# Twelve of the 36 modulation chunks of part one move into the third feed-forward of part two

## The reference, cut to what matters

```python
cond_x = silu(c); cond_c = silu(c_ctx)
mx = split((cond_x @ mod_w[layer] + mod_b[layer])[:, None, :], 9, axis=-1)
mc = split(cond_c @ mod_w[layer] + mod_b[layer], 9, axis=-1)
x  = x  + 0.5 * mx[2] * swiglu(modulate(rms_norm(x),  mx[0], mx[1]), ffn_w_in[layer, 0], ffn_w_out[layer, 0])
xc = xc + 0.5 * mc[2] * swiglu(modulate(rms_norm(xc), mc[0], mc[1]), ffn_w_in[layer, 0], ffn_w_out[layer, 0])
# then the mixer with mx[3..5], then the second feed-forward with mx[6..8]
```

## Time and profile before

| | |
|---|---|
| median of 3 executions | 2864.19 us (2854.37 to 2866.15) |
| the profiled execution: its time, its span | 2856.93 us, 2855.1 us |
| PE busy | 2663.7 us (93%) |
| DVE busy | 1565.7 us (55%) |
| ACT busy | 1078.3 us (38%) |
| HBM read | 390.54 MB, 137 GB/s over the span |
| mean granted TensorE clock | 0.974 |
| part one | about 0 to 1020 us |
| unit (1, 0) | about 2080 to 2460 us |

### The profile page before, as it was taken

One profiled execution on the slowest core, in us unless ns is written; L12 is line 12 of the kernel. 1 busy time (PEld: TensorE's weight loads), 2 busy tenths in 40 slices (PEclk: granted clock), 3 DMA queues, 4 the chain that ended last, 5 costly groups with the idle time before them and its releaser, 6 DMA issues.

```text
span 2855.1 us, 44372 instructions
## 1 busy us (share of the span) xinstructions
PE 2663.7 (93%) x17820; PEld 2325.0 (81%) x17820; DVE 1565.7 (55%) x2307; ACT 1078.3 (38%) x1427; POOL 0.2 (0%) x4
## 2 busy tenths in 40 slices
PE   7999999999999969999998999999999999887997
PEld 6887899888789968877786688787888778876997
DVE  7676665677666564333366553333353423676665
ACT  3354553335455443222241433222232222345443
POOL 0000000000000000000000000000000000000000
PEclk9999999999999989999999999999999999999998
DMA  7655567564557734344432024354534444531563
GB/s 212 198 165 192 177 210 215 154 193 156 188 167 222 213 105 122 106 132 128 133 96 74 1 60 126 106 144 114 145 98 125 139 116 112 114 80 53 144 188 103
DMA packets 591271, 394.54 MB, mean 138 GB/s; under 512 B 52278, under 2 KB 584660, under 8 KB 590932
## 3 DMA queue, kind: packets, MB, share of 16 engines
q1 hardware_dynamic: 591060, 391.63, 47.9%
HBM read 390.54 MB, written 1.05 MB: 137 GB/s over the span
## 4 chain that ended last, share of the span: by engine, by line
PE 76%; DVE 13%; ACT 5%; issue 3%; DMA 2%; DVEq 0%; SPq 0%; ACTq 0%
PE bank L2044 76%; DVE w_lo L1205 4%; ACT w_hi L853 3%; DMA raw<-in_ffn_w_out 2%; DVE xs L1220 1%; DVE t L1220 1%; DVE t L1217 1%; DVE small L1839 1%; DVE h_lo L1220 1%; DVE gates L1213 0%; ACT xs L857 0%; ACT t L857 0%; DVE acc L1213 0%; ACT x_hi L857 0%; DMA raw<-in_w_in 0%
## 5 line engine op out<-in xcount | busy, mean ns | idle before, releaser
L1205 DVE TENSOR_TENSOR w_lo<-raw,w_hi 128x2048 fp32r<-128x2048 f32 (+3 forms) x337 | 687.3, 2040 | 575.8 <-ACT w_hi L853 573.8
L853 ACT CAST w_hi<-raw 128x2048 fp32r<-128x2048 f32 (+3 forms) x337 | 572.9, 1701 | 771.0 <-PE bank L2044 386.7
L2044 PE MATMUL bank<-h_hi,w_hi 128*128 128x512 f32 (+1 forms) x1688 | 590.5, 350 | 25.9 <-DVE h_lo L1220 14.2
L2044 PE MATMUL bank<-h_lo,w_hi 128*128 128x512 f32 (+1 forms) x1688 | 583.1, 345 | 0.0
L2044 PE MATMUL bank<-h_hi,w_lo 128*128 128x512 f32 (+1 forms) x1688 | 582.2, 345 | 0.0
L2044 PE MATMUL bank<-x_hi,w_hi 128*128 128x256 f32 x1344 | 387.8, 289 | 35.8 <-DVE x_lo L1220 13.1
L2044 PEld LDWEIGHTS bank<-h_hi,w_hi 128*128 128x128 f32 x1688 | 321.1, 190 | 79.5 <-issue 23.3
L2044 PE MATMUL bank<-x_lo,w_hi 128*128 128x256 f32 x1344 | 378.8, 282 | 0.0
L2044 PE MATMUL bank<-x_hi,w_lo 128*128 128x256 f32 x1344 | 378.3, 281 | 0.0
L2044 PEld LDWEIGHTS bank<-h_hi,w_lo 128*128 128x128 f32 x1688 | 321.1, 190 | 39.0
L2044 PEld LDWEIGHTS bank<-h_lo,w_hi 128*128 128x128 f32 x1688 | 321.4, 190 | 37.6
(11 more groups left out here) (282 smaller groups left out, 3622.8 us busy)
## 6 DMA issues: line engine op xcount, KB each, us to landing
raw<-in_ffn_w_in SPq DMA_DIRECT2D x176, 512.0 KB
raw<-in_ffn_w_out SPq DMA_DIRECT2D x64, 704.0 KB
raw<-in_w_in SPq DMA_DIRECT2D x40, 1024.0 KB
xs<-in_mod_w SPq DMA_DIRECT2D x36, 1024.0 KB, 7.3
raw<-in_mod_w SPq DMA_DIRECT2D x36, 1024.0 KB
raw<-in_w_ff_in SPq DMA_DIRECT2D x32, 1024.0 KB
raw<-in_w_ff_out SPq DMA_DIRECT2D x32, 1024.0 KB
raw<-in_w_out SPq DMA_DIRECT2D x8, 1024.0 KB
```

Of the source, the lines that this page charges most:

```text
L853: act.copy(w_hi[s][:, w], raw[at % SLOTS][:, w]).then_inc(hi_made, c.did(hi_made))
L1205: dve.tensor_tensor(w_lo[s][:, w], raw[r][:, w], w_hi[s][:, w].bitcast(F32), ALU.subtract).then_inc(lo_made, c.did(lo_made))
L2044: ins = pe.transpose(o, l, r) if transpose else pe.matmul(o, l, r, start=start, stop=stop)
```

## The change

Unit (1, 0) makes twelve modulation chunks in each of its two passes, where it made six, and part one makes twelve in each of its two passes, where it made eighteen. The twelve that move are columns 24 to 35 of layer 1's modulation (in chunks of 256), which the last feed-forward uses. In part one the rest follow each other by three weight chunks (later nine and eight) and the turns come after chunks 23 and 53. In unit (1, 0) a pass now has modulation chunks after k = 1, 2, 3, 4, 5, 6, 8, 10, 12, 14, 15 and 16, and turns after 7 and 18. It had them after 1, 3, 5, 7, 13 and 15 and a turn after 17. Two semaphore counts per pass of part one follow.

```diff
-MOD_AFTER = [6, 8, 10, 13, 16, 18, 20, 22, 24, 26, 28, 30, 32, 34, 40, 42, 44, 47]
+MOD_AFTER = [6, 9, 12, 15, 18, 21, 24, 27, 30, 33, 42, 50]
 MODS1 = len(MOD_AFTER)
-MOD_TURN = (20, 32, 50)
-MOD_GROUPS1 = [(0, 12, 0), (0, 12, 6), (1, 6, 24)]
+MOD_TURN = (23, 53)
+MOD_GROUPS1 = [(0, 12, 0), (0, 12, 6)]
...
-FFN_MOD_AFTER = [1, 3, 5, 7, 13, 15]
-FFN_MOD_TURN = (17,)
-FFN_MODS = {(0, 0): (6, 0, 24), (0, 1): (6, 1, 0), (1, 0): (6, 1, 12), (1, 1): (0, 0, 0)}
+FFN_MOD_AFTER = {0: [], 6: [1, 3, 5, 7, 13, 15], 12: [1, 2, 3, 4, 5, 6, 8, 10, 12, 14, 15, 16]}
+FFN_MOD_TURN = {0: (), 6: (17,), 12: (7, 18)}
+FFN_MODS = {(0, 0): (6, 0, 24), (0, 1): (6, 1, 0), (1, 0): (12, 1, 12), (1, 1): (0, 0, 0)}
...
-        if k in FFN_MOD_AFTER[:FFN_MODS[unit][0]]:
-            out.append(("mod", FFN_MOD_AFTER.index(k)))
+        if k in FFN_MOD_AFTER[FFN_MODS[unit][0]]:
+            out.append(("mod", FFN_MOD_AFTER[FFN_MODS[unit][0]].index(k)))
...
-                        if k in FFN_MOD_TURN[:count // MOD_GROUP]:
+                        if k in FFN_MOD_TURN[count]:
                             mod_turn()
-                        if k in FFN_MOD_AFTER[:count]:
-                            q = FFN_MOD_AFTER.index(k)
+                        if k in FFN_MOD_AFTER[count]:
+                            q = FFN_MOD_AFTER[count].index(k)
```

More of the change, by code:

```diff
@@ L416 @@
             'chunk_used': 72,
-            'd_free': 70,
-            'd_full': 52,
+            'd_free': 63,
+            'd_full': 51,
             'exp_made': 22,
@@ L435 @@
             'm_lo_made': 4,
-            'mod_full': 18,
-            'mod_in': 288,
+            'mod_full': 12,
+            'mod_in': 192,
             'o_hi_made': 9,
@@ L1775, in mod @@
                     for g in range(count // MOD_GROUP):
-                        if k == FFN_MOD_TURN[g]:
+                        if k == FFN_MOD_TURN[count][g]:
                             mod_columns(layer, j, count, first + MOD_GROUP * g)
-                    if k in FFN_MOD_AFTER[:count]:
-                        mod_row(FFN_MOD_AFTER.index(k))
+                    if k in FFN_MOD_AFTER[count]:
+                        mod_row(FFN_MOD_AFTER[count].index(k))
                 def unit_lo(t):
```

## The result

The changed kernel takes 2995.16 us in the median (2994.89 to 3001.81) where the kernel before takes 2862.15: the ratio is 1.0461, with a 95% interval of 1.0441 to 1.0482. The profiled execution took 3001.81 us, with a span of 3000.0, 144.9 us more than the 2855.1 before.

The account below looks back on a forecast made before the run. It took PE as the bound, with loads waiting for slots freed by modulation products. Stalls, clock and moved work, less 2.0 us of old stalls and 12 us in part one, gave +139.3 us: 3003.5 us, range 2950 to 3040.

Parts of the forecast that it names:

- gate/up stalls: Unit (1, 0), mid-chunk: PE waits for an up tile's bank, 5.25 us, five times in each of two passes, 52.5 us.
- chunk 13's: Unit (1, 0), chunk 13: PE waits for a bank evicted behind M14's `w_lo`, 3.4 us, twice, 6.8 us.
- output stalls: Output part of unit (1, 0): PE waits for the residual, 9.4 us, twice in each pass, 37.6 us.
- Clock: PE slower after gaps in unit (1, 0): fourteen stalls by 2.8 us, 39.2 us, plus 1.6 us for two short stalls.
- The check value: Sign that the prediction is right: granted clock of the changed unit (1, 0) near 0.85 in place of 1.00.
- The moved work: Unit (1, 0): twelve more products, 13.2 us of PE, and two more turns, 2.4 us.
- Part one: Twelve products and two turns leave part one: 12 us saved, with bounds of 6 and 34.
- lower of the prediction's own bounds: Whole kernel: 2964 us if the low bounds of clock, loads and part one all fall together.
- the clock stays: Rival, 12%: the stalls in unit (1, 0) come but cost no clock; 2963 us.
- only output steps stall: Rival, 5%: in unit (1, 0) the up tiles' banks come free in time; 2923 us.
- nothing stalls: Rival, 6%: the load is issued before the modulation product ends in unit (1, 0), not slower; 2868 us.
- faster: Rival, 5%: no stall, and part one's waits vanish with their clock; 2846 us, from a saving of 30 us there.

Follow-up runs that it names:

- the run with filler work: Changed kernel with 22 unread matmuls before each of ten waiting up tiles and 40 before each of four output tiles: 2958.97 us, ratio 1.0331.
- the run with places alone: Kernel before, the six products per pass of unit (1, 0) moved to chunks 1 to 6, turn after 8: 2936.46 us, ratio 1.0258.
- the kernel with the later loads: A modulation chunk's load one place later: on the changed kernel (third feed-forward) 2864.67 us; on the kernel before (all three feed-forwards) 2855.10 us; which is meant isn't said.

## Why the prediction was right, point by point

**Idle time.** The sum had 52.5 + 37.6 + 6.8 - 2.0 = 94.9 us; the unit's idle time grew by 101.2 - 6.4 = 94.8. The agreement to 0.1 us is luck: the gate/up stalls came out 3.4 us longer than said, and chunk 13's 2.8 and the output stalls 0.5 shorter. The ten gate/up stalls were 5.59 us each in place of 5.25: the loads on the chain took 5.24 to 6.53 us, mean 5.73, with SP's issue ahead of them, more than the 5.4 derived from the earlier trace rows; PE's last matmul ended 0.3 us later than I had put it, which gave a part of that back. The output stalls were 9.27 in place of 9.4. Chunk 13's were 1.98 in place of 3.4. There the releaser that the profile names can't be the cause, as PE's row and two of DVE show:

```profile
2250.90 0.47 PE L2044 MATMUL bank<-un_hi,w_hi 128*128 128x512 f32 x1 [2.08 <-DVE w_lo L1205]
```
```profile
2248.39 1.63 DVE L1205 TENSOR_TENSOR w_lo<-raw,w_hi 128x1408 fp32r<-128x1408 f32 x1 [0.72 <-ACT w_hi L853]
2250.11 0.69 DVE L1213 TENSOR_TENSOR t<-bank,t 128x512 f32<-128x512 f32 x1
```

The `w_lo` ended at 2250.02, 0.9 us before PE's start; the eviction behind it ended at 2250.80 and PE started 0.10 later. So it is the bank, as the prediction had it. The cast of M14 began at 2246.98, 11.4 us after the product at 2235.60, in place of the 12.4 that it counted.

The Trainium skill (DMA: Bandwidth & Descriptors, Anatomy of one DMA) gave an estimate of 4.4 us for the load on another issuing path, and of ten stalls some 10 us lower in all. The chain's 5.24 to 6.53 us decide for the rows.

**Clock.** 40.8 us were said, 2.8 for each of fourteen stalls and 1.6 for the two short ones. The changed unit shows 36.4, the run with filler work 36.2, and the ten gaps of the run with places alone 2.7 each. The mean of nine older gaps was a fair price, if a little high: 4.4 us over all gaps. The stretches of 10 us behind the two short gaps have the clock at 0.83, so 1.7 us lost for each of them, and about 2.4 are left for each of the fourteen long ones. The check value was badly chosen: I named a clock "near 0.85" for the unit, and it is 0.89. That figure averages over idle time too, in which the clock is low for a part, so it doesn't say how much work is lost.

The Trainium skill (TensorE: Matmul & The Clock Gate, HAM oscillation) describes the bursts from which 0.8 us each was estimated, a sum 28 us lower. This case doesn't bear that price out: 36.4 / 16 is 2.3 us per gap.

**The moved work.** 13.2 + 2.4 = 15.6 us said, 16.0 measured in two pairs of kernels.

**Part one.** 12 us said; 12.3 by the mean of eleven traces, though the one pair of profiled executions shows 7.9. So near a hit is luck, but the reason given holds: PE's busy time falls by 13.0 us in the mean, about the price of twelve products, and its idle time doesn't. Of the waits around the up-projections the prediction said that they would move and not go; so it is, the product at 193.63 waits 2.88 us where that at 201.83 waited 3.68. Overlooked were the 3.6 us of unit (0, 0).

**The sum.** 147.2 for the unit, -12.3 and -3.6 make 131.3, against 133.0 between the medians. The forecast's 139.3 is too high by the clock (4.4), unit (0, 0) (3.6) and little else. The profiled execution of the changed kernel was 6.6 us above its own median, and its part behind the unit took 395.3 us against 385.5; the other kernels, whose code there is the same, have 386.8 to 392.7, so no step of the change is behind that. The lower of the prediction's own bounds doesn't follow from its terms: they give about 2960 and not 2964. Nothing else hangs on it.

**The rivals.** That the clock stays falls with 0.89 and the run with filler work; that only output steps stall, with the ten waits at line 1213; that nothing stalls, with the issue at 2119.54, 1.13 us after the product's start, as at 2134.80. The rival "faster" asked for a first part that gives back more than 30 us. It gives 12 to 21.

## What to carry to other kernels

A ring of load slots and a ring of result banks, served by engines that work in program order, are one loop: count how many places back the slot comes free and how many forward the bank is wanted, and the room between them is the slack, whatever the mean DMA share says. An item with little work behind it (a modulation chunk is 1 MB like a weight chunk, but 1.0 us of PE against 11.0) that holds its slot until that work is done should be loaded after the next weight chunk, if it is wanted no earlier; here that one change of order was worth 130 us, and 8 us in the kernel before. And a gap of PE is priced with the slow matmuls behind it: here each 5 to 9 us of idle time cost 2 to 3 us more.

## What was not expected of the hardware

- Loads of one size differ by turns: successive weight chunks of 1 MB on the chain took 5.38, 6.05, 5.24, 6.53 and 5.30 us, and in the second pass 5.56, 6.38, 5.45, 5.91 and 5.48. The longer ones, the second and the fourth, stand at the same places in both passes. What makes them so wasn't tried.
- A gap needn't be long to cost clock, and its length alone doesn't decide. In the kernel before PE waits 2.36 us, resumes at 1406.56, and from 1407.87 on its matmuls start 0.43 us apart; in the changed kernel gaps of 2.08 and 1.88 us are followed by such slow matmuls too. The gap of 1.49 us was not the earlier trace rows, nor was one of 2.12 us in the kernel with the later loads, at 2436.63. Behind these short gaps PE at first runs at full speed; in the gap of 9.36 us the clock had fallen before PE started again.
- Matmuls whose results nobody reads keep the clock at 1.00 over the unit, through fourteen waits that they fill, and the kernel is 36 us faster for doing more work. As a remedy it is the worst of the three: removing the wait gives 130 us.
